# The RWKV recurrence of a two-block model on one core: a new order of TensorE's products, and copies and sums moved between engines

## What is computed

```python
def _rwkv7_step(S, inp):
    r, w, k, v, kk, b = inp
    sa = jnp.einsum('bhvk,bhk->bhv', S, kk)
    S = S * w[:, :, None, :] - sa[..., None] * b[:, :, None, :] + v[..., None] * k[:, :, None, :]
    return S, jnp.einsum('bhvk,bhk->bhv', S, r)

def _rwkv_bidir(rin, S0_f, S0_b):
    r, decay, kd, v, kk, bd = rin
    S_f, y_f = lax.scan(_rwkv7_step, S0_f, (r, decay[:, :, 0], kd[:, :, 0], v, kk, bd[:, :, 0]))
    S_b, y_b = lax.scan(_rwkv7_step, S0_b, (r, decay[:, :, 1], kd[:, :, 1], v, kk, bd[:, :, 1]),
                        reverse=True)
    return S_f, S_b, y_f + y_b
```

## Time and profile before

| | |
|---|---|
| median of three runs | 4226.95 us (4222.52 to 4227.44) |
| span of the profiled execution | 4224.4 us |
| TensorE busy | 3971.7 us (94%) |
| VectorE, ScalarE, GpSimd busy | 2271.0 us (54%), 1547.2 us (37%), 763.6 us (18%) |
| first RWKV stage, 2172.86 to 2522.20 us | 349.3 us |
| second RWKV stage, 3475.16 to 3816.00 us | 340.8 us |

### The profile page before, as it was taken

How to read it: one execution, slowest core, us unless ns; L and a number is a source line. 1 busy time by engine, 2 the same in 40 slices (tenths; PEclk the granted TensorE clock), 3 DMA queues, 4 the chain that set the end, 5 groups by cost and what they waited for, 6 DMA issues and landing times.

```text
span 4224.4 us, 86296 instructions
## 1 busy us (share of the span) xinstructions
PE 3971.7 (94%) x36672; PEld 2364.7 (56%) x36672; DVE 2271.0 (54%) x3937; ACT 1547.2 (37%) x2591; POOL 763.6 (18%) x953
## 2 busy tenths in 40 slices
PE   8999899899999999999989989899999988998998
PEld 4444875444444444555558876664454437886663
DVE  5773456687343123577544335557678653344556
ACT  2221565200000011233235556663234225556762
POOL 0001311000110000010123332240001114332240
PEclk9999999999999999999999999999999989999999
DMA  4432012344341554344443211222345442222231
GB/s 131 137 111 80 2 71 101 119 145 138 124 155 58 190 184 137 107 170 151 172 140 85 72 53 63 78 82 95 105 162 173 172 150 71 71 60 69 75 103 69
DMA packets 349565, 468.01 MB, mean 111 GB/s; under 512 B 55383, under 2 KB 252791, under 8 KB 348224
## 3 DMA queue, kind: packets, MB, share of 16 engines
q1 hardware_dynamic: 298176, 266.26, 20.5%
q0 software_dynamic: 51008, 196.23, 13.3%
HBM read 328.14 MB, written 147.86 MB: 113 GB/s over the span
## 4 chain that ended last, share of the span: by engine, by line
PE 84%; DVE 6%; ACT 4%; issue 3%; DVEq 1%; DMA 1%; POOL 0%; POOLq 0%; ACTq 0%; SPq 0%
PE psum L492 22%; PE psum L1081 13%; PE psum L708 12%; PE psum L3527 11%; PE psum L2734 5%; PE psum L2750 4%; PE psum L463 3%; PE psum L2720 3%; PE psum L3065 2%; PE psum L2037 1%; ACT arena L2796 1%; PE psum L3569 1%; ACT arena L2817 1%; PE psum L2756 1%; PE psum L433 1%
## 5 line engine op out<-in xcount | busy, mean ns | idle before, releaser
L492 PE MATMUL psum<-arena 128*128 128x512 f32 x2352 | 1030.4, 594 | 8.5 <-DVEq L222 3.6
L492 PEld LDWEIGHTS psum<-arena 128*128 128x128 f32 x2352 | 444.5, 190 | 553.5 <-issue 538.0
L3527 PE MATMUL psum<-arena 64*64 64x64 f32 (+7 forms) x16704 | 539.0, 242 | 58.2 <-issue 33.7
L1081 PE MATMUL psum<-arena 128*128 128x512 f32 x1344 | 583.4, 595 | 9.4 <-DMA arena<-w_down 3.9
L708 PE MATMUL psum<-arena 128*128 128x512 f32 x1232 | 536.7, 596 | 5.9 <-POOLq L222 3.8
L3527 PEld LDWEIGHTS psum<-arena 64*64 64x64 f32 (+2 forms) x16704 | 463.1, 142 | 128.3 <-issue 68.2
L1081 PEld LDWEIGHTS psum<-arena 128*128 128x128 f32 x1344 | 254.6, 191 | 328.3 <-issue 319.2
L708 PEld LDWEIGHTS psum<-arena 128*128 128x128 f32 x1232 | 232.6, 190 | 303.3 <-issue 293.0
L2847 DVE CUSTOM_DVE_ANT_0 arena<-psum,arena 128x512 f32<-128x512 f32 (+3 forms) x532 | 293.4, 591 | 195.1 <-PE psum L2734 189.1
L2796 ACT COPY arena<-psum 128x1024 f32<-128x1024 f32 (+3 forms) x290 | 244.9, 844 | 177.8 <-PE psum L2720 171.6
L2734 PE MATMUL psum<-arena 64*128 64x512 f32 (+3 forms) x1192 | 257.6, 524 | 13.5 <-DVE arena L2847 10.1
(11 more groups left out here) (398 smaller groups left out, 4706.4 us busy)
## 6 DMA issues: line engine op xcount, KB each, us to landing
arena<-w_in SPq DMA_DIRECT2D x86, 512.0 KB, 5.6
proj<-arena SPq DMA_DIRECT2D x172, 256.0 KB, 2.0
arena<-w_mod POOLq DMA_DIRECT2D x24, 1024.0 KB, 5.7
arena<-down_sum SPq DMA_DIRECT2D x40, 512.0 KB, 3.7
arena<-proj POOLq DMA_DIRECT2D x31, 640.0 KB, 5.2
arena<-proj SPq DMA_DIRECT2D x28, 640.0 KB, 7.0
arena<-w_down SPq DMA_DIRECT2D x30, 512.0 KB, 3.8
x_home<-arena POOLq DMA_DIRECT2D x26, 512.0 KB, 3.2
```

Of the source, the lines that this page charges most:

```text
L492: ins = pe.matmul(ps[:, b, :], L[:, k, :], R[:, k, :], start=(p in ("P1", "P5", "P6", "P7") and k == 0), stop=(k == KT // 2 - 1), skip_gro ...
L1081: ins = pe.matmul(self.bank(j, b), self.left(p, j, left, *g)[:, k - g[0], :], R[:, k - k0, :], start=(x in ("P1", "P5", "P6", "P7") and k ...
L3527: return pe.matmul(out, lhsT, rhs, start=first, stop=last, skip_group_check=not (first and last))
```

## The change

It moves products in the list and in the calls. `z` goes behind `y1` of the next pass; the `Q` part of `G` is made between them, as 24 quarter products in place of 12 half ones, and takes its slot before `z`. `tK` and `tB` go behind `xT2`. `H`, `x0` and `S2` go between `x4` and `y5`, and `tV` before `x5`. It moves work between engines: `Z` from GpSimd to VectorE for every chunk, `Hc` from VectorE to GpSimd, and one half of the copies of `x5` from ScalarE to VectorE. `y6` is copied to the room of `U`.

```diff
         self.prod = [p for n in range(-1, NCH + 1) for p in self.order(n)]
-        self.place = {p: i for i, p in enumerate(self.prod)}
+        self.turns = list(self.prod)
+        for n in range(NCH):
+            self.turns.remove(f"G@{n}")
+            self.turns.insert(self.turns.index(f"z@{n}"), f"G@{n}")
+        self.place = {p: i for i, p in enumerate(self.turns)}
+        self.copies = [p for p in self.prod if self.on_act(p)]
+        for n in range(NCH - 1):
+            self.copies.remove(f"z@{n}")
+            self.copies.insert(self.copies.index(f"xT0@{n + 1}") + 1, f"z@{n}")
...
+    def on_dve(self, p):
+
+        return p[:3] == "x5@" or not self.on_act(p)
...
-        out = mine("y1 xT0") + past("G") + mine("x1 S0") + mine("RB1", rows) + mine("y2 xT1") + past("U") + mine("x2 S1 y3 xT2") + past("P0") + mine("x3")
...
-        out += later("L0 L1") + mine("y4 xT3") + past("P1") + mine("x4")
-        out += mine("y5 xT4") + past("H", inv) + later("x0") + mine("RB0", rows) + mine("x5 xT5")
-        return out + mine("S2 y6 tV tK tB z")
+        out = mine("y1") + past("z") + mine("xT0") + past("G") + mine("x1 S0") + mine("RB1", rows) + mine("y2 xT1") + past("U") + mine("x2 S1")
+        out += mine("y3 xT2 tK tB") + past("P0") + mine("x3") + later("L0 L1") + mine("y4 xT3") + past("P1") + mine("x4")
+        out += past("H", inv) + later("x0") + mine("S2 y5 xT4") + mine("RB0", rows)
+        return out + mine("tV x5 xT5 y6")
...
+            if n > 0:
+                pool.wait_ge(Dv.sem, Dv.at(0, f"H@{n - 1}"))
+                pool.tensor_tensor(hex6(b["Hc"]), hex6(b["H"]), self.fc[:, n, :].unsqueeze(2).broadcast_to([P, 6, 64]), ALU.mult).then_inc(s.sem, 1)
...
-                Z = flat12(b["Z"])
...
-                if m:
-                    pool.tensor_tensor(Z, flat12(b[f"AT{m % 2}"]), twelve(self.c.const("negT64")), ALU.mult)
-                    pool.drain()
-                    pool.tensor_tensor(Z, Z, ident, ALU.add).then_inc(s.sem, 1)
...
-                old = self.prod[i - 4]
-                st = A if self.on_act(old) else Dv
-                pe.wait_ge(st.sem, st.at(0, old))
+                old = self.turns[i - 4]
+                if self.on_act(old):
+                    pe.wait_ge(A.sem, A.at(0, old))
+                if self.on_dve(old):
+                    pe.wait_ge(Dv.sem, Dv.at(0, old))
...
+        def state_q(n):
+            st = O if n else Dv
+            pe.wait_ge(st.sem, st.at(0, f"Hc@{n}"))
+            out = start(f"G@{n}")
+            for i, (d, j) in enumerate(pairs):
+                for c, p in ((0, 0), (1, 1), (1, 0), (0, 1)):
+                    mm(out[HALF[c], p, 64 * i:64 * i + 64], head("Q", d, p, j, n)[:, HALF[c]], sq("Hc", p, 0, i),
+                       first=(i == 0), last=False)
...
-            pe.wait_ge(Dv.sem, Dv.at(0, f"Hc@{n}"))
...
-            out = start(f"G@{n}")
-            for i, (d, j) in enumerate(pairs):
-                for p in range(2):
-                    mm(out[:, p, 64 * i:64 * i + 64], head("Q", d, p, j, n), sq("Hc", p, 0, i), first=(i == 0), last=False)
+            out = self.bank(f"G@{n}")
...
+                if state and l == 1:
+                    state_q(n - 1)
+                    joined(n - 1)
+                if inv:
...
+                if inv and l == 3:
+                    turn(n, "K")
+                    turn(n, "B")
...
-                if state and inv and l == 5:
-                    state_h(n - 1)
-                if n + 1 < NCH and l == 5:
-                    inverse_first(n + 1)
...
+                if state and inv and l == 4:
+                    state_h(n - 1)
+                if n + 1 < NCH and l == 4:
+                    inverse_first(n + 1)
+                if inv and l == 4:
+                    key_scores(n, 2)
             if inv:
-                key_scores(n, 2)
                 join(n)
-                for x in "VKB":
-                    turn(n, x)
-                joined(n)
...
-        for name in self.prod:
-            if not self.on_act(name):
-                continue
...
-                for f in range(2):
-                    act.copy(F[HALF[f], :, 1:6:2, HALF[f]], ps[HALF[f], 1, :].rearrange("p (a j t) -> p a j t", a=2, j=RT))
-                    ins = act.copy(hex6(self.part(f"X{n % 2}", f))[HALF[f], 0:6:2, :], tri(ps[HALF[f], 0, 192 * f:192 * f + 192]))
+                act.copy(F[HALF[0], :, 1:6:2, HALF[0]], ps[HALF[0], 1, :].rearrange("p (a j t) -> p a j t", a=2, j=RT))
+                ins = act.copy(hex6(self.part(f"X{n % 2}", 0))[HALF[0], 0:6:2, :], tri(ps[HALF[0], 0, 0:192]))
             elif p == "y6":
                 for q in range(2):
                     f = HALF[1 ^ q]
-                    ins = act.copy(self.part("Y", q)[f, :], ps[f, q, :])
+                    ins = act.copy(self.part("U", q)[f, :], ps[f, q, :])
...
-        dve.wait_ge(A.sem, A.at(0, "L1@0"))
-        dve.tensor_tensor(Z, flat12(b["AT0"]), bits("negT64"), ALU.mult)
-        dve.drain()
-        dve.tensor_tensor(Z, Z, bits("ident64"), ALU.add).then_inc(s.sem, 1)
...
-            if self.on_act(name):
+            if p == "x0":
+                dve.wait_ge(A.sem, A.at(0, f"L1@{n}"))
+                dve.tensor_tensor(Z, flat12(b[f"AT{n % 2}"]), bits("negT64"), ALU.mult)
+                dve.drain()
+                dve.tensor_tensor(Z, Z, bits("ident64"), ALU.add).then_inc(s.sem, 1)
+            if not self.on_dve(name):
...
-            elif p == "xT5":
+            elif p == "x5":
...
+                F = b["F"].rearrange("p (a i t) -> p a i t", a=2, i=6)
+                dve.tensor_copy(F[HALF[1], :, 1:6:2, HALF[1]], ps[HALF[1], 1, :].rearrange("p (a j t) -> p a j t", a=2, j=RT))
+                ins = dve.tensor_copy(hex6(self.part(f"X{n % 2}", 1))[HALF[1], 0:6:2, :], tri(ps[HALF[1], 0, 192:384]))
+            elif p == "xT5":
...
+                if n:
+                    dve.wait_ge(O.sem, O.at(0, f"Hc@{n}"))
...
-            if p == "H":
-                dve.wait_ge(s.sem, s.at(0, name))
-                dve.wait_ge(O.sem, O.at(0, "fc"))
-                dve.tensor_tensor(hex6(b["Hc"]), hex6(b["H"]), by64(self.fc[:, n + 1, :]), ALU.mult).then_inc(s.sem, 1)
```

More of the change, by code:

```diff
@@ L3375, in __init__ @@
         self.s_pe = Steps(core.pe, self.prod, 1)
-        self.s_act = Steps(core.act, [p for p in self.prod if self.on_act(p)], 1)
-        dve = ["Hc@0", "Z@0"]
+        self.s_act = Steps(core.act, self.copies, 1)
+        dve = ["Hc@0"]
         for p in self.prod:
-            if not self.on_act(p):
+            if p[:3] == "x0@":
+                dve.append(f"Z@{p[3:]}")
+            if self.on_dve(p):
                 dve.append(p)
-            if p[:2] == "H@":
-                dve.append(f"Hc@{int(p[2:]) + 1}")
         self.s_dve = Steps(core.dve, dve, 1)
@@ L3385, in __init__ @@
         for n in range(-1, NCH):
-            pool += [f"M{l}@{n}" for l in range(2, 6) if n >= 0] + [f"Z@{n + 1}"] * (0 <= n < NCH - 1) + [f"M1@{n + 1}"] * (n + 1 < NCH)
+            pool += [f"M{l}@{n}" for l in range(2, 6) if n >= 0] + [f"Hc@{n}"] * (n > 0) + [f"M1@{n + 1}"] * (n + 1 < NCH)
             pool += ["F", "fc"] if n < 0 else []
@@ L3446, in sp @@
                 if n > 0:
-                    sp.wait_ge(E.sem, E.at(0, f"tB@{n - 1}"))
+                    sp.wait_ge(E.sem, E.at(0, f"tV@{n - 1}"))
                 self.load(sp, n + 1, "KBV", 0)
@@ L3469, in run_pool @@
         b, s, E, A, Dv = self.b, self.s_pool, self.s_pe, self.s_act, self.s_dve
-        ident, lev = twelve(self.c.const("ident64")), lambda l: twelve(self.c.const("levT64", l))
+        lev = lambda l: twelve(self.c.const("levT64", l))
         for n in range(-1, NCH):
@@ L3500, in run_pool @@
                 ins.then_inc(s.sem, 1)
+                pool.drain()
     def run_pe(self, pe):
@@ L3577, in inverse_first @@
         def inverse_first(n):
-            st = O if n else Dv
-            pe.wait_ge(st.sem, st.at(0, f"Z@{n}"))
+            pe.wait_ge(Dv.sem, Dv.at(0, f"Z@{n}"))
             turn_half(f"x0@{n}", "Z")
@@ L3599, in join @@
             pe.wait_ge(A.sem, A.at(0, f"x5@{n}"))
+            pe.wait_ge(Dv.sem, Dv.at(0, f"x5@{n}"))
             out = start(f"y6@{n}")
@@ L3615, in joined @@
                         if d == 0:
-                            ins = mm(out[HALF[p], p, 64 * i:64 * i + 64], sq("Y", f, p, i), full(p)[HALF[f], i, HALF[f]])
+                            ins = mm(out[HALF[p], p, 64 * i:64 * i + 64], sq("U", f, p, i), full(p)[HALF[f], i, HALF[f]])
                         else:
-                            ins = mm(out[HALF[f], p, 64 * i:64 * i + 64], sq("XT", f, p, j), sq("Y", f, p, i))
+                            ins = mm(out[HALF[f], p, 64 * i:64 * i + 64], sq("XT", f, p, j), sq("U", f, p, i))
             ins.then_inc(s.sem, 1)
@@ L3718, in run_pe @@
                     state_u(n - 1)
+                if inv and l == 3:
+                    turn(n, "K")
+                    turn(n, "B")
```

(11 more changed lines are left out.)

2 lines of the change are left out of this document (removed).

## The result

The change made the kernel slower. Its median is 4291.65 us (4286.13 to 4292.5, 4 runs) against 4225.32 us before (4222.52 to 4227.44, 4 runs): ratio 1.0148, 95% interval 1.0136 to 1.0161. The prediction said 4265 us, slower, with a range of 4230 to 4289: the direction came true, and the time lies 27 us above the number and 3 above the range. The profiled execution spans 4284.3 us, 59.9 more than the one before.

The account below looks back on a forecast made before the run. TensorE was taken to set the pace of the two RWKV stages. Middle passes +21, first and last passes -10 and the clock +27 sum to +38 us on 4227: 4265 us, range 4230 to 4289.

Parts of the forecast that it names:

- `x0`'s wait: TensorE waits 3.3 us at `x0`, behind `H`, for VectorE to make `Z`, in each of 16 passes.
- The pair: VectorE's two operations making `Z`, behind its sum `H`: 2.6 us beside GpSimd's `Hc`, bounds 2.0 and 3.5.
- The third rival: VectorE and GpSimd don't collide at `Z`; `x0` waits 2.7 us, the clock holds: +2 us; 8%.
- The clock: TensorE's clock falls to half behind `x0`'s wait in 13 or 14 of 16 passes, 2.0 us each: +27 us.
- The second rival: TensorE's clock holds despite the wait at `x0`: 4238 us; 14%.
- The fifth rival: Half clock lasts and makes the next waits longer: 16 x 3.5 us or more, above 4289; 6%.
- The fourth: Waits only shift, `y6` and `S0` don't wait, and relieving ScalarE is worth something: 4227 us; 6%.
- `y6` and `S0`: New TensorE waits in a pass: 0.5 us at `y6` for `x5`'s copies, 0.35 us at `S0` for `G`'s slot.
- The waits at `y5` and `tB`: Old TensorE waits for a copy and a slot, forecast to go: 1.20 and 0.43 us a pass.
- First and last passes: Passes without `H` or next `x0` get faster, about 3.5 us each first, 1.5 each last: -10 us together.
- The `Q` part: `Q` part of `G` as 24 quarter products, 48 instructions, takes 0.57 us less a pass; bounds 0 and 0.6.
- 16 x 1.3 for the waits: Net of 4.15 us of new waits less 2.8 us saved, in 16 passes with `H` and next `x0`: +21 us.

Follow-up runs that it names:

- e1: Changed kernel with `x0`, and with it VectorE's pair of operations for `Z`, ahead of `H`: 4237.57 us, ratio 1.0005 to 1.0028 to the kernel before.
- e2: Changed kernel with GpSimd's `Hc` also waiting for VectorE's next `Z`: 4282.71 us, ratio 1.0106 to 1.0140 to the kernel before.
- e8: Changed kernel with `x0` ahead of `H`, `Q` part as halves, `tK` and `tB` behind `y6`: 4214.81 us, ratio 0.9963 to the kernel before.
- e9: As e8, but `tK` ahead of `y6` and `tB` behind it: 4219.41 us, ratio 0.9970 to 0.9987 to the kernel before.
- e10: Kernel before, with only the `Q` part of `G` as quarter products: 4238.70 us, ratio 1.0016 to 1.0040.
- e3: Changed kernel with the `Q` part of `G` again as 24 half products: 4288.38 us, ratio 1.0112 to 1.0150 to the kernel before.
- e11: Kernel before, with `H` and `x0` ahead of `y5`, `Z` still made by GpSimd: 4245.82 us, ratio 1.0025 to 1.0053.
- e5: Changed kernel with `x0` ahead of `H` and the `Q` part as halves: 4222.45 us, ratio 0.9975 to 0.9993 to the kernel before.
- e6: As e1, with `tK` and `tB` behind `y6` and the next chunk's loads waiting for `tB`: 4229.39 us, ratio 0.9992 to 1.0010 to the kernel before.
- run 72: Not a follow-up run: the words belong to "in the dense run 72 products start within 1.1 us", the dense run being the stretch of quarter products on TensorE.
- e7: As e1, with the next chunk's data loads waiting for `U` in place of `tV`: 4254.22 us, ratio 1.0046 to 1.0073 to the kernel before.

## Where the prediction was right, and where it was short

**`x0`'s wait: right.** 3.3 us were forecast, from the last issue of `H`; the trace shows 3.24 (3.02 by the row's count), in each pass. The pair was to last 2.6 us and lasts 2.51, from 2381.89 to 2384.40. e1 shows that it is the stall that costs, e2 that VectorE and GpSimd hold each other up. The Trainium skill, "SBUF — State Buffer", "SBUF: two separate sides", would have the three operations run whole, one behind the other, 2.75 us from the durations of e2's rows; 2.51 is 0.24 less, so the rows agree with its rule in kind and not in full. The third rival (no collision, 8%) is out.

**The clock: right in the sum.** 13 or 14 passes at 2.0 us were forecast, 27 in all. It fell in 15, for 68 us; at 1.5 us for each 3.41 us that is some 30 us (an estimate from the passes above). So more passes fell, and a fall cost less, than was said. The second rival (the clock holds, 14%) is out, though one pass shows the clock holding behind the same stall. e1 removes the stall and leaves 17 us in five stretches, each 1 to 2 us behind the end of a standstill of 1.4 to 2.9 us; four gaps of 2.5 to 2.9 us have none behind them. e8, without stall and long gaps, has none. The fifth rival (half clock makes the next waits longer, above 4289) has the time but not the cause: 13 of the 16 stretches last only 3.41 us, and one costs 1.5, not 3.5. The fourth (waits only shift, 6%) is out by the time.

**`y6` and `S0`: right.** 0.5 and 0.35 us were forecast; the rows show 0.53 at `y6` in each pass, and before `S0` 0 to 0.5, 0.18 on average, beyond the change of shape. The waits at `y5` and `tB` are gone. e9 adds that hiding `y6`'s wait by a transpose brings nothing.

**First and last passes: right**, -10 us were forecast; it is 8.8 within the stages, and 10.2 as the difference of 70.1 and 59.9.

**The `Q` part: wrong, in sign.** "The `Q` part ... as 24 quarter products it is 48 instructions ...: 0.57 less" counted what the instructions take once they are there. The bounds were 0 and 0.6; a loss wasn't among them. e10 shows the form alone making the old kernel slower by 0.28% (0.16% to 0.40%), and e3 that taking it back removes 23 of the changed kernel's 30 us of gaps. The saving was there in part; the gaps weren't in the sum. I had also counted the joined run of quarters as a gain ("two shape changes fewer").

The sum closes with this, if the forecast's own terms are taken for the rest: 16 x 1.3 for the waits, 27 for the clock and 22.3 for the gaps (29.8 less 7.5) give 70.4 for the passes, where 70.1 were measured. That isn't a test of the first two terms. With the 30 us estimated for the clock, 18 are left for the waits, in place of 21. The term that was missing is the 22.3, most of the 27 us by which the forecast was short.

The same can be done for e1. By standstills over 0.5 us that do end with a semaphore (76.5 us in the changed kernel's passes, 27.0 in e1's) it gains 49.5. Eight of them, 4.5 us, are no waits but a load at half clock ahead of `y5`, so 45. The clock gives 22 (51 us less at half, at 1.5 for 3.41), and the gaps take 11: 56 in all, where its passes gained 53. Gaps of less than 0.5 us aren't in my count.

**A sentence that was wrong without harm:** "GpSimd had made `Z` long ahead". In the trace of before it ended 0.7 us ahead of `x0`, and e11 waits for it.

**Why do the gaps come?** The experiments show that they grow with the number of instructions packed into a stretch (e3, e5, e6, e8, e10). What they wait for stands in the DMA view. One pass of e1, from 2374.9 to 2408.3 us, shows 7 packets on the instruction queue:

```profile
q8 instruction: 7, 0.11, 1.6%
```

That is 16 KB each, one in 4.8 us. Three signs in the traces tie the gaps to these packets:

- Where a gap ends. All 211 gaps in the passes of the 13 traces end 1.2 to 1.7 us after a packet of this queue has landed, while the packets start some 4.2 us apart (the median in e1's passes).
- Where a gap lies. Count TensorE's instructions from one gap of a stage to any other, products, loads of weights and semaphore instructions together: it is a whole multiple of 256 in every case, in all 13 traces. The passes of e1 have 31415 such instructions and 124 packets, 253 for each. So the gaps lie only where one packet's instructions end and the next one's begin.
- What the two rates are. 256 instructions hold some 128 products. In the dense run 72 products start within 1.1 us, so one packet is used up in about 2. The shortest distance between two packets' starts is 3.2 to 3.5 us in each of the 13 traces.

Three of e1's gaps, in us:

| gap | packet | from its end to the gap's |
|---|---|---|
| 2282.15 to 2285.04 | 2281.63, takes 2.04 | 1.37 |
| 2382.99 to 2385.53 | 2382.68, takes 1.45 | 1.40 |
| 2418.66 to 2421.50 | 2418.76, takes 1.40 | 1.34 |

So TensorE stands because its next instructions haven't come. How long it stands would then depend on how far the packets had run ahead of it when the run began, which also fits the larger gaps of e1, where no stall lets them run ahead; that part is argued. What sets the distance between packets, and how much of it is due to data loads (e7), no run here isolates.

## What to carry to other kernels

Before an operation is given to an engine that has time, look at what stands ahead of it in that engine's order, and who waits behind: the same pair made TensorE stand 3 us a pass behind `H` and not at all ahead of it. A product cut into more, smaller instructions must be paid for in instructions too: count how many a stretch packs together, look for idle time inside products that is put down to issue, and see whether it ends behind a packet on the instruction queue. And take such a change apart before dropping it: with `x0` first, `Q` in halves and two transposes in the dense run, the rest of it made the kernel 0.37% faster (0.23% to 0.50%) than before.

## What was not expected of the hardware

- TensorE stands inside a product, with nothing to wait for, for 0.5 to 3.1 us, where many small instructions stand together: 20 times in 16 passes of the changed kernel, 6 times in e8's.
- It does so at every 256th instruction only (products, loads and semaphore instructions counted), and starts again 1.2 to 1.7 us after a packet of 16 KB on the instruction queue has landed: 211 of 211 gaps.
- 24 more products of 64x64 a pass, of about 1000, took these gaps from 7.5 to 24.4 us in the kernel before, and from 6.4 to 29.8 in the changed one.
- With the data loads moved out of the stretch the longest gap was 1.8 us in place of 2.9 (e7, e1); a new wait came with it, so the share of the loads is open.
- A stretch of 3.41 us at half clock cost 1.5 us; one stall of 16 just as long was followed by full clock.
- VectorE's and GpSimd's operations with both inputs in SBUF hold each other up: 0.96 and 0.83 us apart, 1.42 and 1.48 together.
